# Expert stage of a hybrid decoder step: two sets of banks for the down products, one wider block last, gathers issued together

## The reference, cut to what matters

```
out[b] = (silu(x[tok] @ w1[e]) * (x[tok] @ w3[e])) @ w2[e]      # one block b of tokens of expert e
y      = zeros.at[slot_tok].add(out * slot_w)                    # back to the tokens, weighted
x      = layer_norm(alpha * x + y)
```

## Time and profile before

| what | us |
|---|---|
| median of 3 runs (1465.8 to 1469.98) | 1466.87 |
| the profiled execution, its time | 1473.97 |
| its span | 1472.1 |
| PE busy (share of the span) | 1368.9 (93%) |
| DVE busy | 671.2 (46%) |
| POOL busy | 566.1 (38%) |
| ACT busy | 309.4 (21%) |
| mean granted TensorE clock | 0.969 |

### The profile page before, as it was taken

One profiled execution on the slowest core, in us unless ns is written; L12 is line 12 of the kernel. 1 busy time (PEld: TensorE's weight loads), 2 busy tenths in 40 slices (PEclk: granted clock), 3 DMA queues, 4 the chain that ended last, 5 costly groups with the idle time before them and its releaser, 6 DMA issues. The chain is left out here.

```text
span 1472.1 us, 33644 instructions
## 1 busy us (share of the span) xinstructions
PE 1368.9 (93%) x13661; PEld 960.7 (65%) x13661; DVE 671.2 (46%) x1362; ACT 309.4 (21%) x843; POOL 566.1 (38%) x452
## 2 busy tenths in 40 slices
PE   8999999998998999999999858999999989999864
PEld 4678888865566668887777534666666766666641
DVE  4757787842325567666667471112112111111127
ACT  1311011113113444443443100011001001100015
POOL 4212423402223235543334012445545544445435
PEclk9999999999998999999999979999999999999987
DMA  6334333244136232213321199999999999999936
GB/s 250 89 97 99 76 78 102 61 121 160 47 110 245 90 100 80 86 66 115 115 94 44 72 396 376 388 399 399 396 396 404 395 395 398 395 395 395 392 87 237
DMA packets 129606, 318.04 MB, mean 216 GB/s; under 512 B 48120, under 2 KB 86512, under 8 KB 103672
## 3 DMA queue, kind: packets, MB, share of 16 engines
q1 hardware_dynamic: 109720, 294.35, 53.3%
q0 software_dynamic: 18656, 18.15, 5.7%
q10 hardware_dynamic: 1152, 4.52, 0.8%
HBM read 277.05 MB, written 47.74 MB: 221 GB/s over the span
## 5 line engine op out<-in xcount | busy, mean ns | idle before, releaser
L2660 PE MATMUL bank<-sb_arena 128*32 128x256 f32 x6144 | 341.5, 381 | 12.2 <-DVE sb_arena L2768 5.7
L2660 PEld LDWEIGHTS bank<-sb_arena 128*32 128x32 f32 x6144 | 222.9, 111 | 125.4 <-issue 13.2
L515 PE MATMUL bank<-sb_arena 128*128 128x276 f32 x1008 | 235.0, 395 | 0.0
L2631 POOL DMA_INDIRECT d_acc<-sb_arena,sb_oidx x96 | 152.1, 1584 | 194.0 <-ACT sb_arena L2726 166.0
L515 PEld LDWEIGHTS bank<-sb_arena 128*128 128x128 f32 x1008 | 191.0, 190 | 44.0
L2676 PE MATMUL bank<-sb_arena 128*32 128x256 f32 x3072 | 172.9, 379 | 7.7 <-ACT sb_arena L2726 7.6
L2676 PEld LDWEIGHTS bank<-sb_arena 128*32 128x32 f32 x3072 | 110.6, 110 | 66.4 <-ACT sb_arena L2726 9.9
L2624 POOL DMA_INDIRECT sb_arena<-d_x,sb_idx x99 | 102.6, 1037 | 109.4 <-DVE sb_idx L2754 51.8
L2773 DVE TENSOR_SCALAR sb_oidx<-sb_slot 128x3 int32 x32 | 5.6, 174 | 286.1 <-DMA d_acc<-sb_arena,sb_oidx 285.7
L2726 ACT ACTIVATE sb_arena<-bank,sb_arena 128x256 f32<-128x256 f32 x96 | 38.5, 472 | 397.1 <-DVE sb_arena L2774 387.7
L1281 PE MATMUL bank<-sb_arena 128*128 128x512 f32 (+1 forms) x256 | 119.7, 596 | 0.0
(11 more groups left out here) (420 smaller groups left out, 1842.5 us busy)
## 6 DMA issues: line engine op xcount, KB each, us to landing
sb_arena<-w SPq DMA_DIRECT2D x192, 1024.0 KB, 28.1
sb_arena<-w_conv SPq DMA_DIRECT2D x28, 512.0 KB, 4.8
sb_arena<-d_conv SPq DMA_DIRECT2D x7, 1792.0 KB, 7.3
d_conv<-sb_arena SPq DMA_DIRECT2D x22, 512.0 KB, 3.3
sb_arena<-d_gam SPq DMA_DIRECT2D x8, 768.0 KB, 5.2
d_x<-sb_arena SPq DMA_DIRECT2D x9, 512.0 KB, 2.6
sb_arena<-xT ACTq DMA_DIRECT2D x8, 552.0 KB, 9.3
sb_arena<-w_out SPq DMA_DIRECT2D x8, 512.0 KB, 7.9
```

What stands on the lines that cost most here:

```text
L515: last = e.matmul(bank[at + t][:, 0:HT // 2], weights[:, k, :], x[:, k, HT // 2 * t:HT // 2 * t + HT // 2], start=(k == 0), stop=(k == HK ...
L2631: e.indirect_dma_start(rows_out, bass.IndirectOffsetOnAxis(ap=oidx[:, r:r + 1], axis=0), eo[:, r, :], None, bounds_check=LAST_ROW, oob_is_ ...
L2660: mm = e.matmul(bank[UPB + r][j * CG:(j + 1) * CG, 0:2 * P], xgT[:, 2 * q + k, r * CG:(r + 1) * CG], w13[s][q][:, k, j, :], start=(q == 0 ...
```

## The change

It has these parts:
1. **Down products to two sets of banks in turn** (4 and 5, 6 and 7; unit 2 has the second half of unit 0's bank). down(n) waits for the evictions of block n-2. Units 0 and 1 are made first, then unit 2; a w2 half is told free after unit 2 has used it. TensorE's loop has six bodies (four passes), five more are written out, one loop and a last down follow.
2. **One block of four units last.** The expert with 97 to 128 tokens gets one block of 128 slots at the last position (31 here); its fourth unit is gathered early to `xg_end`. Its down products are 16 passes of 128 x 512 columns, for all four units at once. VectorE's gate of it stands behind mark(30), ScalarE's tanh behind evict(30).
3. **Gathers together:** all three of a position wait for `e_idx` alone.
4. **VectorE's order:** h_flip(b) ahead of mark(b-1).
5. **Routing** makes fewer lists; part of the work moves ahead of the first count.
6. **Early weights:** three quarters of expert 0's w1 and w3 are loaded in the mixer stage; the buffers `ch` and `spread` move to the arena's start for that.
7. **d_acc's rows** are loaded by SP at the end of the expert stage, when the scatters of the block before the last have landed.

The diff's core:

```diff
@@ SP, mixer stage
                 for i in range(1, NTT + 2):
+                    if i == 2:
+                        for c in range(4):
+                            e.wait_ge(S[f"ch_st{c}"], 32)
+                        e.wait_ge(S["ss_ps"], 8)
+                        for q in range(EARLY):
+                            e.dma_start(early[q], a["w13"][0, q]).then_inc(W["w13" + "abcd"[q] + "0"], 16)
@@ SP, routing
-                    for q in range(4):
+                    for q in range(EARLY if s == 0 else 0, 4):
@@ VectorE, routing, behind the counts
-                step(e.tensor_tensor(count, upto_t[:, :, NTT - 1], star, ALU.add))
...
-                step(e.tensor_scalar(nblk, rowi[:], 1.0, None, ALU.max))
...
+                step(e.scalar_tensor_tensor(over, count, float(WIDE), over, ALU.is_le, ALU.mult))
...
+                step(e.scalar_tensor_tensor(el, before_t, float(BLK), bc1(shift, P, NTT, E), ALU.is_ge, ALU.mult))
+                e.tensor_tensor(before_t, before_t, el, ALU.add).then_inc(S["r_before"], 1)
@@ the lists: 42 instructions go, these come
+                step(e.tensor_scalar(swapped, wide_of[0:1, 0:1], 1.0, None, ALU.min))
+                step(e.tensor_scalar(swapped, swapped, -float(E1), float(E1), ALU.mult, ALU.add))
+                step(e.tensor_tensor(end_of, swapped, wide_of[0:1, 0:1], ALU.add))
+                for t in (source, order):
+                    e.scalar_tensor_tensor(t[0:1, 0:E1], iota[0:1, 0:E1], end_of[0:1, 0:1], iota[0:1, 0:E1], ALU.is_ge, ALU.add)
+                e.tensor_tensor(cmp_, bc1(row[6][0:1], 1, NX, E), bc(turn, 1, NX, E), ALU.is_le).then_inc(S["r_v"], 1)
+                e.tensor_scalar(is_end, turn, total, None, ALU.is_equal)
...
+                step(e.tensor_reduce(oexp, cmp_, AX, ALU.add))
+                step(e.scalar_tensor_tensor(oexp, turn, total, oexp, ALU.is_lt, ALU.mult))
+                e.scalar_tensor_tensor(source[0:1, E1:NBMAX], is_end, end_of[0:1, 0:1], oexp, ALU.mult, ALU.add)
@@ banks
-        UPB, LAST, OUT = 0, 3, 5
+        UPB = 0
+        OUT = [4, 6]
+        def out_of(side, r):
+            return bank[OUT[side] + r % 2][:, 256 * (r // 2):256 * (r // 2 + 1)]
@@ SP, end of the expert stage
+                e.wait_ge(S["e_st"], 48 * last + 16)
+                for t in range(NTT):
+                    n = m_of(t)
+                    e.dma_start(rows[t][0:n], a["d_acc"][row_of(t):row_of(t) + n, :]).then_inc(LOADED[t], 16)
@@ POOL
-                    gather(n, apart=True)
+                    gather(n)
@@ TensorE
-                def down(n, s, load):
+                def down(n, s, load, side, evicted):
                     e.wait_ge(S["e_hT"], n + 1)
                     for r in range(NR):
-                        e.wait_ge(S[f"e_eo{r}"], n + 3)
+                        e.wait_ge(S[f"e_eo{r}"], evicted)
+                    for units in ((0, 1), (2,)):
+                        for h in range(2):
...
+                            for k in range(2):
+                                c = 2 * h + k
+                                for r in units:
+                                    for j in range(4):
+                                        mm = e.matmul(out_of(side, r)[j * CG:(j + 1) * CG], hT[:, c, r * CG:(r + 1) * CG], w2[s][h][:, k, j * 256:(j + 1) * 256],
+                                                      start=(c == 0), stop=(c == 3))
+                            if units == (2,):
+                                mm.then_inc(S["e_out"], 1)
...
+                with nc.Fori(0, (E2 - 2) // SIX, engines=bass.OrderedEngineSet([e.engine]), hint_back_edge=True) as i:
+                    for j in range(SIX):
...
+                with e.Fori(E2, last) as b:
                     up(b, UP_SET, b)
+                    down(e.snap(b - 1), DOWN_SET, b, (E2 - 1) % 2, e.snap(b + 2))
+                down(e.snap(last - 1), UP_SET, E2 // NSET + 1, E2 % 2, E2 + 2)
...
+                        for d in range(2):
+                            mm = e.matmul(bank[UPB + d][:, :], hT[:, c, :], w2[END_SET][h][:, k, d * 512:(d + 1) * 512], start=(c == 0), stop=(c == 3))
@@ ScalarE, end
+                evict(e.value_load(ends[0:1, 0:1], min_val=E1 - 1, max_val=REST - 2), E2 % 2)
+                tanh(last, units=NR + 1)
@@ VectorE
                     gate(b)
+                    h_flip(b)
                     mark(e.snap(b - 1))
-                    h_flip(b)
+                e.wait_ge(S["e_x_end"], 16)
+                e.transpose(xgT[:, :, BLK:WIDE], xg_end.rearrange("p (k b) -> p k b", b=CG))
                 x_flip(last)
                 gate(before)
+                h_flip(before)
                 mark(two_before)
-                h_flip(before)
-                gate(last)
                 mark(before)
-                h_flip(last)
+                gate(last, units=NR + 1)
+                h_flip(last, units=NR + 1)
@@ SP, last stage
-                for t in range(NTT):
-                    n = m_of(t)
-                    e.dma_start(rows[t][0:n], a["d_acc"][row_of(t):row_of(t) + n, :]).then_inc(S[f"c_in{t:02d}_"], 16)
```

More of the change, by code:

```diff
@@ L787, in program @@
         A = Arena()
+        early = [A(P, KT * 2 * P) for _ in range(EARLY)]
+        A = Arena()
+        ch = [A(P, SB, P) for _ in range(4)]
+        spread = [A(TS, SB, P) for _ in range(2)]
+        assert A.at == EARLY * KT * 2 * P
         cv = [A(P, CT, P) for _ in range(2)]
@@ L828, in program @@
         lnc = A(P, 4)
-        ch = [A(P, SB, P) for _ in range(4)]
-        spread = [A(TS, SB, P) for _ in range(2)]
         DIAG = SB * (QUAD + SL)
@@ L2282, in program @@
         before_t = A(P, NTT, E)
-        row = [A(P, E) for _ in range(10)]
+        row = [A(P, E) for _ in range(8)]
         NX = NBMAX - E1
         cmp_ = Arena(one_hots_at)(1, NX, E)
-        oexp, oseq, is_extra, is_main, is_part, behind = [A(1, NX) for _ in range(6)]
-        part_of = A(P, 1)
-        one = [A(1, 1) for _ in range(6)]
-        span_, moved, pick_main = [A(1, E) for _ in range(3)]
-        listed = A(P, 2, NBMAX + 2)
+        oexp, oseq, is_end = [A(1, NX) for _ in range(3)]
+        wide_of = A(P, 1)
+        swapped, end_of = [A(1, 1) for _ in range(2)]
+        first_at = A(P, 2, NTT)
         dest = A(P, 2, NTT)
@@ L2360, in _ @@
                                         listed[0:BLK, :, 0:NBMAX], start=True, stop=True)
+                last = e.matmul(bank[4][BLK:WIDE, 0:2].rearrange("p (a n) -> p a n", a=2), ident[0:BLK, 0:CG], listed[0:BLK, :, REST:NBMAX], start=True, stop=True)
                 last.then_inc(S["r_pe"], 1)
@@ L2368, in _ @@
                 e.memset(xg, 0.0)
+                e.memset(xg_end, 0.0)
                 e.memset(eo, 0.0)
@@ L2423, in _ @@
                 step(e.tensor_tensor_scan(upto_t.rearrange("p e t -> p (e t)"), later_t.rearrange("p e t -> p (e t)"), bank[1][:, 0:NTT * E], 0.0, ALU.mult, ALU.add))
-                count, nblk, end, first = row[0], row[1], row[2], row[3]
-                step(e.scalar_tensor_tensor(over, upto_t[:, :, NTT - 1], float(BLK), number, ALU.is_gt, ALU.mult))
-                step(e.tensor_reduce(part_of, over, AX, ALU.max))
-                step(e.tensor_scalar(star, number, part_of[:, 0:1], float(PAD), ALU.is_equal, ALU.mult))
@@ L2429, in _ @@
-                step(e.tensor_tensor(count, upto_t[:, :, NTT - 1], star, ALU.add))
+                count, until, xblk = upto_t[:, :, NTT - 1], row[6], row[7]
+                step(e.scalar_tensor_tensor(over, count, float(BLK), number, ALU.is_gt, ALU.mult))
+                step(e.scalar_tensor_tensor(over, count, float(WIDE), over, ALU.is_le, ALU.mult))
+                step(e.tensor_reduce(wide_of, over, AX, ALU.max))
+                step(e.tensor_scalar(star, number, wide_of[:, 0:1], None, ALU.is_equal))
@@ L2509, in _ @@
[L2509 to L2513 removed]
+                turn, total = iota[0:1, 0:NX], row[6][0:1, E - 1:E]
+                step(e.tensor_scalar(swapped, wide_of[0:1, 0:1], 1.0, None, ALU.min))
@@ new lines, in _ @@
+                e.tensor_scalar(table[0:1, 0:1], total, float(E1), None, ALU.add)
+                for k in range(2):
+                    e.tensor_scalar(ends[0:1, k:k + 1], total, float(E1 - 1 - k), None, ALU.add)
+                e.tensor_scalar(order[0:1, NBMAX:NBMAX + 4], iota[0:1, 0:4], 0.0, float(NBMAX), ALU.mult, ALU.add)
+                done[0] += 1
+                step(e.scalar_tensor_tensor(oseq, turn, total, iota[0:1, E:E + NX], ALU.is_lt, ALU.mult))
+                e.scalar_tensor_tensor(order[0:1, E1:NBMAX], is_end, end_of[0:1, 0:1], oseq, ALU.mult, ALU.add)
@@ L2680, in _ @@
-                idle_products(e, bank[7][:, :], 8)
-                up(0, 0, 1, first=True)
-                with nc.Fori(0, (E - 2) // NSET, engines=bass.OrderedEngineSet([e.engine]), hint_back_edge=True) as i:
-                    for j in range(NSET):
-                        before, s = e.snap(NSET * i + j), (j + 1) % NSET
```

(23 more changed lines are left out.)

246 lines of the change are left out of this document (113 added, 133 removed).

## The result

The changed kernel takes 1486.07 us (median of 4 runs, 1482.02 to 1487.14) beside 1466.62 of the kernel before (1465.80 to 1469.98): ratio 1.0123, 95% interval 1.0098 to 1.0148. Forecast were 1458.0 and a range of 1449 to 1467, with 0.13 for slower. The profiled execution has a span of 1483.8 us and a time of 1485.65.

A forecast was written before the change was run, and what follows sets the result against it. The ring of evictions, scatter-adds and marks was taken to set the pace. Terms before the end summed to -5.8 us; with the end, the last stage starts 9.0 us earlier, taking 1466.87 to 1457.9, forecast 1458.0, range 1449 to 1467.

The forecast's parts named there:

- rival (4): TensorE's six-body loop is fetched anew each pass; at 1 us a block 1496 us, deciding from 0.4; chance 0.13.
- the ring: Expert stage: evictions, scatter-adds, their landing and VectorE's mark, with one buffer, set the pace at 16.38 us a turn.
- The stops at the jumps back: TensorE's three jumps back: stops of 3.4 + 1.5 us each, 15 in all, hidden by its lead; cost 0 to 5.
- Two sets of banks, 0: Down products in the expert stage: some 4 us more slack for TensorE, nothing off the ring; 0 us directly.
- Gathers, -2.0: POOL, 28 turns: without two waits, the late third gather's 3.00 us TensorE stop goes; -2.0 us, bounds -2.0 and 0.
- First turn, -0.9: First turn: scatter(0) no longer behind the third gather, but mark(0) 1.1 us later; -0.9 us, bounds -2.0 and 0.
- Routing, -1.9: VectorE's routing stage: fewer small instructions in place of 8.45 us of them; -1.9 us, bounds -0.5 and -3.
- Early weights, -1.0: First position: its third gather holds the flip less without weights beside it; -1.0 us, bounds -3.2 and 0.
- The end: Expert stage's end: mark(30) at 1406.0, down(31) done 1418.5, d_acc loads issued by 1419.9; last stage starts 9.0 us earlier, 1424.3.
- Loads of d_acc ahead, 0: Last stage: its first sum waited for TensorE, not the loads, so nothing gained inside; 0 us, bounds -1 and 0.

The follow-up runs named there:

- the six-body run: The kernel before with TensorE's loop of six bodies in place of three, same instructions in the same order: 1495.57 us, ratio 1.0175.
- The runs with three bodies: The changed kernel with TensorE's loop of three bodies: 1474.17 us with one set of banks, 1459.9 with two, 1459.6 to 1462.11 in three variants of the latter.
- the written-out one: The kernel before with TensorE's thirty bodies written out, no loop and no jump back: 1493.96 us, ratio 1.0165.
- the kernel with three bodies and two sets: The changed kernel with a loop of three bodies, given bank sets 0, 1, 0, the last two positions written out: 1459.9 us, ratio 0.9938.
- three bodies and one set: The changed kernel with one set of banks for all down products and a loop of three bodies: 1474.17 us, ratio 1.0036.

## Why the prediction was wrong

**The step that failed: rival (4), "The code no longer stays".** The rule was named, the trace had its first half, and the rival was even given its deciding size: "0.4 us a block". From the six-body run and the kernel before it is (420.86 - 392.22) us of turns over the blocks of those 24 turns, about 2.5 a turn (15 a pass, where the prediction has 12): 28.6 / 60 = 0.48 us a block. I looked for this cost on the wrong engine. I asked whether a block stops TensorE, found "six fetches in the first pass without a stop" and took that as evidence against. But TensorE has slack there; the ring has none, and the ring's link through DMA is what a fetch lengthens. Its 0.13 was far too low; its time, 1496, is that of the six-body run by luck: it came from 48 stops of TensorE of 1 us, less 10 of slack, and a stop at each block is in none of the runs.

The trace of before showed it in a place that I read otherwise. Its last full landing, 10.7 (mark at 1400.61), stands exactly where q8 fetched again; I took it for a trait of "the latest turns". (Its first two landings, 9.4, stand in the first pass, but turns 18 to 23 have up to 9.9 with no fetch.) The runs with three bodies show it within one kernel: 9.0 on average in turns 4 to 17, 8.8 in turn 25, and from turn 26, where the written-out positions begin, 10.4, 10.3, 10.6 and 10.8.

The stops at the jumps back were foreseen (3.4 and 1.5 us, hidden; measured 4.2 to 4.6 and 0.9 to 1.5, hidden).

The Trainium skill, page "Runtime: NRT & Kernel Launch", section "Instruction fetch mechanics", calls the cost of crossing a block "mostly hidden", and gives the stall at a taken branch out of "the current 2-page window" as a reason to prefer full unrolling. The trace agrees that TensorE is hardly stopped by a block (3.3 us in 440 when written out). But the loop of three bodies, six blocks long by the earlier trace rows, jumped back without a fetch or a stop, so here the 128 KiB of the prediction fit and the window doesn't; and the written-out loop is 1.65% slower than it.

**The other terms**, read from the kernel with three bodies and two sets, where code size is out of the way. Its 1459.9 is 1.9 over the forecast, but the kernel before took 1470.5 beside it; the ratio, 0.9938, matches the forecast's 1458.0 / 1466.87 = 0.9940. That match is in part luck. All 9.0 us of the forecast were to come ahead of the last stage. Counted from the end of the mixer, 5.9 came there, for late turns took 5.2 that it lacks, and 2.8 inside the last stage, for which it had no term. The times after the span's start, below, match better than they should: this execution left the mixer 5.3 us earlier (837.2, before 842.5), a spread that the kernel before shows among its own executions.

- *Two sets of banks, 0*: right for the ring (24 turns in 390.55 us; with one set 391.40). At the end I had used them without pricing them: without them it is 14 us slower.
- *Gathers, -2.0*: the turns are 0.5 us shorter than with the gathers apart (390.55 and 391.00), near the zero bound, and the mechanism was wrong. The stop of 3.0 us is still there with the gathers together. First the kernel before, then this one:

```profile
1200.42 1.05 POOL L2624 DMA_INDIRECT sb_arena<-d_x,sb_idx  x1 [7.84 <-issue]
```

```profile
1127.61 1.04 POOL L2646 DMA_INDIRECT sb_arena<-d_x,sb_idx  x1 [7.59 <-issue]
...
1137.48 11.92 PE L2684 MATMUL bank<-sb_arena 128*32 128x256 f32 x192 [3.42 <-DVE sb_arena L2806]
```

It is not the third gather waiting for a product, but the second one standing with no wait that the profile names, until 0.3 us after a mark. The changed kernel and all seven variants of it have this twice, at mark(13) and mark(26), the kernel before once, at mark(17). Each time the ring's next turn is 1.1 to 1.2 us longer than its landing explains (here 17.49 with a landing of 9.16; a turn is its landing and 7.17 elsewhere). What holds the gather isn't shown.
- *First turn, -0.9*: the second mark comes 48.0 us after up(0) starts, before 47.2: +0.8, with a landing of 10.8 where it was 9.4. Putting the mark first again makes it 45.7, but not the kernel faster.
- *Routing, -1.9*: from the mixer's last routing product to up(0) 51.9 to 52.2 us in seven of the eight traces of before's code (50.9 in the other), 49.0 to 49.3 in the new one with three bodies: -2.9, near the good bound (48.1 in the changed kernel itself). That product's end itself lies between 836.8 and 842.5 in the eight traces of before's code, which is the same up to there. The changed kernel's, 835.1, lies 1.7 below them; how much of that is the change isn't shown.
- *Early weights, -1.0*: 0 up to up(0), and not told apart in the time.
- *Late turns*: from the 26th to the 30th mark 71.8 us, before 66.5. These 5.2 us are missing from the forecast: 4.2 are landings, since the two written-out positions are code to be fetched, and 1.0 the second stop of the gathers.
- *The end*: mark(30) 1405.28 (forecast 1406.0), down(31) from 1409.70 to 1418.5 (1411.4 to 1418.5; its 16 products took 8.8 us, not 7.1, at a granted clock of 0.81), the last load of d_acc issued at 1420.7 (1419.9), the last stage from 1422.2 (1424.3). The sum of TensorE's work there counts the 96 products of down(30) for the new kernel alone; without them it is 20.9 us against 20.7, and nothing else hangs on it.
- *Loads of d_acc ahead, 0*: from the last stage's first product to the span's end 35.9 us; 38.8 before. The 2.8 are TensorE's clock and not the loads. The stage's first 28 products, before:

```profile
1433.35 15.30 PE L2864 MATMUL bank<-sb_arena 128*64 128x512 f32 x28 [10.82 <-PEq L157]
```

They took 15.30 us, after 10.8 us without a product; the granted clock was 0.50 (1.2 GHz) for the first 2.7 and 0.59 on average for the next 4.0. Here they took 12.40 at 1.00 (2.4 GHz), after 3.7 us without one. In both kernels 23.5 us are left for the rest of the stage. The same is so with three bodies and one set, where they took 14.05. So the loads are worth 0, as forecast, and the clock is a term that the forecast doesn't have.

In the changed kernel itself down(31) ends at 1445.7 where the forecast had 1418.5: 27 us late, about what the ring lost. The start of the last stage and the stage itself give 6.5 back, so the span is 20.7 over the forecast.

## What to carry to other kernels

In these kernels code size was a DMA load. The loop of three bodies fetched nothing after its first pass. The loop of six took its toll from the ring that waits for the DMA; TensorE, which runs the code, stopped too, but was far enough ahead to hide it. Before doubling a loop body to alternate buffers, count the instruction queue's packets per pass; an uneven pattern (0, 1, 0) in the old body gave the same overlap here. When a cost is ruled out because "the engine didn't stop", ask the same of the link that sets the pace.

## What was not expected of the hardware

- Instruction blocks of 16 KB, one every 7 us (0.9% of 16 engines' time over 500 us, 71 blocks: 1.0 us each), lengthen the landing of an indirect scatter from 9.1 to 10.2 us, while two data loads of the same size a turn (some 0.7 us each) do not in the first 17 turns.
- A load of 16 KB into one partition, twice a position, costs 2.8% of the time; the same bytes over 16 partitions cost 0.6%.
- Eight executions of code that is the same up to there reach the end of the mixer up to 5.8 us apart.
- In the changed kernel and its variants two of GpSimd's gathers, 13 positions apart, stand 7.1 to 9.6 us with no wait that the profile names, and start 0.3 us after a mark.
